# Third block's merge in a three-block kernel on one Trainium2 core: the second branch and the output projection in halves of four tiles, the first tiles in a buffer of their own, the residual totalled on VectorE

## The reference, cut to what matters

```
mixed = (jax.nn.sigmoid(ga) * (h_a @ w_proj_a[layer])
         + jax.nn.sigmoid(gb) * (h_b @ w_proj_b[layer]))
x = _layernorm(ALPHA * x + mixed @ w_out[layer], ln1_g[layer], ln1_b[layer])

ffn = (jax.nn.silu(x @ w_ffn_gate[layer]) * (x @ w_ffn_up[layer])) @ w_ffn_down[layer]
x = _layernorm(ALPHA * x + ffn, ln2_g[layer], ln2_b[layer])
```

## Time and profile before

| | us |
|---|---|
| median of 3 runs | 4739.69 |
| lowest, highest | 4737.83, 4743.4 |
| the profiled execution's own time | 4738.33 |
| its span, first to last instruction | 4736.5 |
| TensorE busy, share of the span | 4343.9, 92% |
| VectorE busy | 2453.9, 52% |
| GpSimd busy | 1295.0, 27% |
| ScalarE busy | 1322.5, 28% |
| mean granted TensorE clock | 0.951 of full |

### The profile page before, as it was taken

How to read it: one execution, slowest core, us unless ns; L and a number is a source line. 1 busy time by engine, 2 the same in 40 slices (tenths; PEclk the granted TensorE clock), 3 DMA queues, 4 the chain that set the end, 5 groups by cost and what they waited for, 6 DMA issues and landing times. The chain is left out here.

```text
span 4736.5 us, 55353 instructions
## 1 busy us (share of the span) xinstructions
PE 4343.9 (92%) x22174; PEld 3377.4 (71%) x22174; DVE 2453.9 (52%) x3774; ACT 1322.5 (28%) x2079; POOL 1295.0 (27%) x502
## 2 busy tenths in 40 slices
PE   8999999978989998989999999989998887988998
PEld 6766787635658784678888678757776775766876
DVE  5544576336647736467777567554552436122023
ACT  3344233213213324223333333222222111102222
POOL 1001443202114330000000144334553331654432
PEclk9999999979999999889999999989998998989999
DMA  5210222212112222510000212211112111211221
GB/s 168 107 36 19 92 103 89 76 71 89 53 71 90 105 96 90 184 56 35 22 35 21 73 71 106 76 72 72 71 71 75 54 54 36 89 71 71 106 89 54
DMA packets 41294, 357.92 MB, mean 76 GB/s; under 512 B 4275, under 2 KB 4659, under 8 KB 21500
## 3 DMA queue, kind: packets, MB, share of 16 engines
q1 hardware_dynamic: 41084, 354.97, 20.6%
HBM read 333.46 MB, written 21.50 MB: 75 GB/s over the span
## 5 line engine op out<-in xcount | busy, mean ns | idle before, releaser
L192 PE MATMUL banks<-ffn_in_high,ffn_weights_low 128*128 128x512 f32 x2112 | 833.0, 394 | 65.3 <-issue 31.7
L193 PE MATMUL banks<-ffn_in_low,ffn_weights_high 128*128 128x512 f32 x2112 | 828.8, 392 | 0.0
L194 PE MATMUL banks<-ffn_in_high,ffn_weights_high 128*128 128x512 f32 x2112 | 828.2, 392 | 0.0
L260 POOL TENSOR_TENSOR ffn_weights_low<-weight_ring,ffn_weights_high 128x2048 fp32r<-128x2048 f32 x128 | 601.2, 4697 | 824.5 <-ACT ffn_weights_high L337 823.8
L192 PEld LDWEIGHTS banks<-ffn_in_high,ffn_weights_low 128*128 128x128 f32 x2112 | 401.4, 190 | 156.1 <-issue 34.4
L193 PEld LDWEIGHTS banks<-ffn_in_low,ffn_weights_high 128*128 128x128 f32 x2112 | 401.1, 190 | 84.8 <-issue 1.5
L194 PEld LDWEIGHTS banks<-ffn_in_high,ffn_weights_high 128*128 128x128 f32 x2112 | 400.7, 190 | 84.2
L337 ACT ACTIVATE ffn_weights_high<-weight_ring 128x2048 fp32r<-128x2048 f32 x128 | 245.1, 1915 | 582.5 <-PE banks L194 582.4
L192 PE MATMUL banks<-third_x_high,third_weights_low 128*128 128x512 f32 x832 | 332.6, 400 | 61.7 <-POOL third_weights_low L3063 24.5
L438 DVE SCALAR_TENSOR_TENSOR ffn_gate<-ffn_up,columns_sb,ffn_gate 128x511 f32<-128x511 f32 (+1 forms) x132 | 287.2, 2176 | 167.6 <-ACT ffn_value L368 167.6
L3063 POOL TENSOR_TENSOR third_weights_low<-weight_ring,third_weights_high 128x1024 fp32r<-128x1024 f32 x144 | 363.2, 2522 | 11.5
(11 more groups left out here) (543 smaller groups left out, 7943.1 us busy)
## 6 DMA issues: line engine op xcount, KB each, us to landing
weight_ring<-weights SPq DMA_DIRECT2D x144, 2048.0 KB, 7.7
scan_in<-rwkv_operands SPq DMA_DIRECT2D x8, 1280.0 KB, 6.8
rwkv_operands<-rwin_staged SPq DMA_DIRECT2D x24, 256.0 KB, 2.1
scan_in<-rwkv_operands SPq DMA_DIRECT2D x8, 512.0 KB, 3.9
bias_tiles<-bias_rows SPq DMA_DIRECT2D x8, 448.0 KB, 8.8
residual<-x SPq DMA_DIRECT2D x4, 512.0 KB, 7.0
filt_decay<-decay SPq DMA_DIRECT2D x1, 2048.0 KB, 8.1
rwkv_residual<-residual SPq DMA_DIRECT2D x1, 2048.0 KB, 7.4
```

The costliest lines, as they stand in the source:

```text
L192: pe.matmul(out, w[1], x[0], start=start, stop=False, skip_group_check=True)
L193: pe.matmul(out, w[0], x[1], start=False, stop=False, skip_group_check=True)
L194: return pe.matmul(out, w[0], x[0], start=False, stop=stop, skip_group_check=True)
L260: pool.tensor_tensor(parts[1], landed, parts[0].bitcast(F32), ALU.subtract).then_inc(S["split"], 1)
```

## The change

Host side: the second branch's weights are laid out by halves of the output columns, four units of 256 rows by 512 columns for each half, and the output projection's by halves of the input rows, four units of 512 rows by 256 columns for each. Number and size of chunks stay.

In `gated_merge`:

- A buffer `merge_early` (high and low part, four tiles each) takes tiles 0 to 3 of branch a and tiles 0 to 3 of the output projection's input. ScalarE and VectorE fill it for branch a at the start of the block, ahead of the gates. Everything else stays in `x_parts`.
- TensorE waits bank by bank, not for all: at the start of branch a for the sigmoid of bank m, at the start of branch b for the multiply of bank m.
- Branch b is two halves of four units. The first half computes output tiles 0 to 3 over all eight input tiles, the second 4 to 7. VectorE takes up the first half's banks as soon as that half is done.
- The output projection is two halves of four units as well. The first takes input tiles 0 to 3 for all eight output tiles, the second input tiles 4 to 7. Its output banks 2j and 2j+1 are finished at the end of unit 4+j.
- VectorE adds the residual tiles up as they are done (seven adds, into the first tile of `merge_gate`), and TensorE sums that one tile with the matrix of ones still inside the merge's block. VectorE waits for this before the block ends.

In `layer_norm` the sum over eight tiles is left out for `ln1`. `ln2` is as before.

```
-            pe.wait_ge(S["gate_done"], 2 * KT)
-            for t in range(tiles):
-                if t == tiles_a:
-                    pe.wait_ge(S["branch_done"], KT)
+            for t in range(tiles_a):
                 pe.wait_ge(S["split"], gate_units + t + 1)
                 pe.wait_ge(S["tile_split"], t + 1)
                 w = w_parts(gate_units + t)
                 for m in range(KT):
-                    mm = exact_product(pe, G.banks[:, m, :], [x[:, m * P:(m + 1) * P] for x in w], [x[:, t % KT, :] for x in x_parts],
-                                       start=t in (0, tiles_a), stop=t in (tiles_a - 1, tiles - 1))
+                    if t == 0:
+                        pe.wait_ge(S["gate_done"], KT + m + 1)
+                    mm = exact_product(pe, G.banks[:, m, :], [x[:, m * P:(m + 1) * P] for x in w], parts(t),
+                                       start=(t == 0), stop=(t == tiles_a - 1))
                 mm.then_inc(S["used"], 1)
-            pe.wait_ge(S["tile_split"], tiles + KT)
-            for m in range(KT):
-                output(gate_units + tiles + m, m)
+            for u in range(KT):
+                half = u // HALF
+                w = [x.rearrange("p (k n) -> p k n", k=2) for x in w_parts(unit_b + u)]
+                pe.wait_ge(S["split"], unit_b + u + 1)
+                for s in range(2):
+                    k = u % HALF * 2 + s
+                    pe.wait_ge(S["tile_split"], tiles_a + k + 1)
+                    for m in range(half * HALF, (half + 1) * HALF):
+                        if k == 0:
+                            pe.wait_ge(S["branch_done"], m + 1)
+                        mm = exact_product(pe, G.banks[:, m, :], [x[:, s, m % HALF * P:(m % HALF + 1) * P] for x in w], parts(tiles_a + k),
+                                           start=(k == 0), stop=(k == KT - 1))
+                mm.then_inc(S["used"], 1)
+            for u in range(KT):
+                w = [x.rearrange("p (k n) -> p k n", k=HALF) for x in w_parts(unit_out + u)]
+                pe.wait_ge(S["split"], unit_out + u + 1)
+                for s in range(HALF):
+                    k = u // HALF * HALF + s
+                    pe.wait_ge(S["tile_split"], tiles + k + 1)
+                    for side in range(2):
+                        m = u % HALF * 2 + side
+                        if k == 0:
+                            pe.wait_ge(S["branch_done"], KT + m + 1)
+                        mm = exact_product(pe, G.banks[:, m, :], [x[:, s, side * P:(side + 1) * P] for x in w], parts(tiles + k),
+                                           start=(k == 0), stop=(k == KT - 1))
+                mm.then_inc(S["used"], 1)
+            pe.wait_ge(S["totalled"], KT - 1)
+            pe.matmul(G.banks[:, 0, :], G.con("ones"), total, start=True, stop=True).then_inc(S["total_summed"], 1)
...
             for m in range(KT):
-                dve.wait_ge(S["used"], gate_units + tiles)
+                dve.wait_ge(S["used"], unit_b + (HALF if m < HALF else KT))
                 dve.tensor_tensor(G.hT[:, m, :], G.banks[:, m, :], G.hT[:, m, :], ALU.mult).then_inc(S["branch_done"], 1)
                 dve.wait_ge(S["branch_done"], KT + m + 1)
                 dve.tensor_tensor(G.hT[:, m, :], G.hT[:, m, :], gates[0][:, m, :], ALU.add).then_inc(S["mixed"], 1)
-            for k in range(KT):
-                tile_low(tiles + k)
+                if m % HALF:
+                    tile_low(tiles + m - 1)
+                if m % HALF == HALF - 1:
+                    tile_low(tiles + m)
             for m in range(KT):
-                dve.wait_ge(S["used"], gate_units + tiles + m + 1)
+                dve.wait_ge(S["used"], unit_out + HALF + m // 2 + 1)
                 dve.scalar_tensor_tensor(out=G.x[:, m, :], in0=G.x[:, m, :], scalar=ALPHA, in1=G.banks[:, m, :],
                                          op0=ALU.mult, op1=ALU.add).then_inc(S["added"], 1)
+                if m:
+                    dve.wait_ge(S["added"], m + 1)
+                    if m > 1:
+                        dve.wait_ge(S["totalled"], m - 1)
+                    dve.tensor_tensor(total, G.x[:, 0, :] if m == 1 else total, G.x[:, m, :], ALU.add).then_inc(S["totalled"], 1)
+            dve.wait_ge(S["total_summed"], 1)
...
-    layer_norm(G, "ln1", "ln1_g", "ln1_b")
+    layer_norm(G, "ln1", "ln1_g", "ln1_b", total_summed=True)
```

More of the change, by code:

```diff
@@ L3631, in gated_merge @@
     nc = G.nc
+    HALF = KT // 2
     tiles_a, tiles_b = M_HEADS * MT_, H_HEADS
@@ L3634, in gated_merge @@
     gate_units = 2 * KT
-    units = gate_units + tiles + KT
+    unit_b = gate_units + tiles_a
+    unit_out = unit_b + KT
+    units = unit_out + KT
     with ExitStack() as ctx:
-        S = stage(G, "merge", ctx, "restored", "rounded", "split", "used", "tile_high", "tile_split", "gate_done", "branch_done", "mixed", "added")
+        S = stage(G, "merge", ctx, "restored", "rounded", "split", "used", "tile_high", "tile_split", "gate_done", "branch_done", "mixed", "added",
+                  "totalled", "total_summed")
         gates = [G.sb("merge_gate", [P, KT, SEQ], ctx=ctx), G.hT]
+        early = [G.sb("merge_early_" + part, [P, HALF, SEQ], F32R, ctx=ctx) for part in ("high", "low")]
+        total = gates[0][:, 0, :]
         x_parts = [T.x_high, T.x_low]
@@ L3646, in source, with parts @@
             return T.haT[:, t, :] if t < tiles_a else T.hbT[:, t - tiles_a, :] if t < tiles else G.hT[:, t - tiles, :]
+        def parts(t):
+            return [x[:, t % KT, :] for x in (early if t < HALF or tiles <= t < tiles + HALF else x_parts)]
         @block.sync
@@ L3659, in _ @@
                     pool.wait_ge(S["used"], n - 1)
[L3660 to L3664 removed]
+                if n >= gate_units:
+                    split_unit(pool, S, G.ring[:, G.slot(c), n % 4 * UNIT:(n % 4 + 1) * UNIT], w_parts(n), n)
+                else:
+                    split_unit(pool, S, column_unit(G, c, n % 4), [w.rearrange("p (k n) -> p k n", k=KT) for w in w_parts(n)], n)
         @block.tensor
         def _(pe):
[L3668 to L3675 removed]
             for t in range(gate_units):
@@ L3679, in _ @@
                     pe.wait_ge(S["gate_done"], t - 7)
[L3680 to L3684 removed]
+                pe.wait_ge(S["split"], t + 1)
+                w = [x.rearrange("p (k n) -> p k n", k=KT) for x in w_parts(t)]
+                for k in range(KT):
+                    mm = exact_product(pe, G.banks[:, t % 8, :], [x[:, k, :] for x in w], [x[:, k, :] for x in x_parts],
+                                       start=(k == 0), stop=(k == KT - 1))
+                mm.then_inc(S["used"], 1)
+            for t in range(tiles_a):
                 pe.wait_ge(S["split"], gate_units + t + 1)
@@ L3698, in tile_high @@
             def tile_high(t):
-                act.activation(x_parts[0][:, t % KT, :], source(t), ACT.Copy).then_inc(S["tile_high"], 1)
+                act.activation(parts(t)[0], source(t), ACT.Copy).then_inc(S["tile_high"], 1)
+            for t in range(HALF):
+                tile_high(t)
             for t in range(2 * KT):
@@ L3706, in _ @@
             act.wait_ge(S["restored"], KT)
-            for t in range(tiles):
+            for t in range(HALF, tiles):
                 if t >= KT:
@@ L3761, in _ @@
         def _(pe):
-            for k in range(KT):
-                mm = pe.matmul(G.banks[:, 0, :], G.con("ones"), G.x[:, k, :], start=(k == 0), stop=(k == KT - 1))
-            mm.then_inc(S["summed"], 1)
+            if not total_summed:
+                for k in range(KT):
+                    mm = pe.matmul(G.banks[:, 0, :], G.con("ones"), G.x[:, k, :], start=(k == 0), stop=(k == KT - 1))
+                mm.then_inc(S["summed"], 1)
             for k in range(KT):
```

22 lines of the change are left out of this document (13 added, 9 removed).

## The result

| us | before | changed |
|---|---|---|
| median, 20 runs each | 4742.09 | 4710.9 |
| lowest, highest | 4731.99, 4748.25 | 4696.99, 4775.71 |
| profiled execution, own time | 4738.33 | 4708.93 |
| span | 4736.5 | 4707.0 |
| ratio, 95% interval | | 0.9949 [0.9928, 0.9969] |

What follows compares the result with a forecast made beforehand. TensorE, busy 92% of the span, was taken as the bound, losing time at stops and slow clock; 5.9 + 6.6 + 18.9 + 2.2 = 33.6 us off 4738.33 gave 4704.7, median 4706, stated 4705; range 4699 to 4711, stretched to 4712.

Steps and rivals of the forecast that it cites:

- Gates to branch a: Joint from gates to branch a: first tiles split early, sigmoid awaited bank by bank, TensorE runs through; minus 5.9 us.
- Branch a to b: Joint from branch a to b: TensorE waits for one multiply, not eight, 0.9 us rest left, no slow start; minus 6.6 us.
- Branch b to output: Joint from branch b to output projection: VectorE and ScalarE finish tiles while the halves run, nothing waits; minus 18.9 us.
- The end: Layer norm's start: one product with ones for eight, earlier mean, part given back in slower squares; minus 2.2 us.
- the least of my three values for the end: At the layer norm, single product and squares both slow: 1.1 us won; the others were 3.9 and 2.2.
- the dear restart: At branch b's start, TensorE restarting slowly after its rest would make the forecast 2.6 us worse.
- GpSimd becoming the bound: Rival: behind the halves, GpSimd's weight splits, slowed beside VectorE, hold TensorE up, up to 5 us; 4710 us, chance 0.10.
- come back at half size: Rival: a tile or bank of the output's first half is late, costing about half of 17.3 us; about 4714 us, chance 0.05.
- fall from lack of rest: Rival: in branch b and output, TensorE without rest drops to clock 0.50; about 4790 us, chance 0.02.

Runs made afterwards that it cites:

- no_early_a: The changed kernel with the early buffer used for the output projection alone, branch a's first four tiles split after the gates; median 4713.56 us.
- b_waits_all: The changed kernel, but TensorE begins branch b only when all eight multiplies are done; 4713.49 us (one run).
- b_whole: The changed kernel with branch b as before (one input tile for all eight outputs) and only the output projection in halves; median 4716.46 us.
- out_waits_all: The changed kernel, but TensorE begins the output projection only when all eight input tiles are split; median 4719.09 us.
- joints_only: The changed kernel with the old layer-norm sum: no adds into a total, eight products with ones inside the layer norm; median 4706.92 us.
- tail_only: The kernel before with only the new end: total on VectorE, one product with ones, none in the layer norm; median 4737.29 us.
- three_products: The changed kernel, but TensorE sums the total of residual tiles 0 to 5, then tiles 6 and 7, with the ones matrix; median 4708.91 us.

## Why the prediction was right and where it was wrong

Three of the four terms were right, mechanism and size; the fourth, the end, was not.

*Gates to branch a* (minus 5.9): 11.38 - 5.44 = 5.94 measured, and its cause by no_early_a.

*Branch a to b* (minus 6.6): 13.00 - 6.57 = 6.43. The rest of 0.9 us is 0.88 in the trace. The products ran at the full clock behind it (1.00 from 4180 to 4184 us), as taken from the rests of 1.04 and 2.17 us. By b_waits_all and the kernel before, the clock is a quarter to a third of what the full wait costs (1.6 of 5.7, 2.6 of 7.6 us).

*Branch b to output* (minus 18.9): 24.38 - 5.44 = 18.94. VectorE's long operations came out longer than the longest I had seen (2.91 us for 2.14) and all of them stayed hidden, four tiles in 15.5 us.

*The end* (minus 2.2) is **the step that failed**: 17.88 us before against 17.97, so nothing won, 0.1 us lost. The wait for VectorE was right (2.83 us for 2.8). The single product ran at the low clock (2.08 us; I had taken 1.0 and kept 2.07 as a bound), the way from its end to the mean took 0.95 us where I had 0.44 from another block's barrier, and the squares took 9.56 us where I had 8.83. These are 1.1, 0.5 and 0.7 us, the 2.3 us between forecast and result. Even the least of my three values for the end, 1.1 us won, was too good by 1.2. With the same end, three profiles (the changed kernel twice, b_whole) have the product at 2.08 us and the end at 17.8 to 18.0; three others (no_early_a, out_waits_all, b_waits_all) have 1.32 to 1.45 us and 16.4. The rest ahead of it was 2.83 us each time, so how much of the product is slow is a matter of when the clock falls, and in the changed kernel the end is worth 0 to 1.5 us. Why it falls earlier in some is open.

Sum: 5.94 + 6.43 + 18.94 - 0.1 = 31.2 us, the measured stretch, where the prediction said 33.6. Its time of 4705 is 5.9 us below the median measured: 2.4 us lie in the stretch, nearly all of it the end, another 2.4 in the kernel before, whose median is 4742.09 over 20 runs and was 4739.69 over the three that I started from, and the last 1.1 in rounding and parts outside the change.

*The range* was made badly too. Its own terms add up to 4700.9 to 4710.3, or 4712.4 with the dear restart, and not to 4699 to 4711. For the runs it allowed 3.7 us above the median, from three runs; the 20 of the changed kernel lie from 14 us below theirs to 65 above. That the median of 4710.9 is inside and the time by the ratio, 4718, outside is decided by these runs and not by the mechanism.

*The rivals.* GpSimd becoming the bound did not happen: after the start of the merge TensorE never waited for a unit. GpSimd's subtract takes 2.75 us beside such operations of VectorE and 2.43 otherwise, VectorE's operation up to 2.91 for 0.68; VectorE pays. The Trainium skill (SBUF — State Buffer, "SBUF: two separate sides") has an exclusive lock on the port pair that the two share, which whoever starts first holds for its whole instruction. The rows agree, with GpSimd as the holder: VectorE's low part that began at 4231.24, 0.39 us after GpSimd's subtract, ended 0.54 us after it, and VectorE's operations are short in out_waits_all where GpSimd has nothing to do. The joint did not come back at half size. The clock did not fall from lack of rest: 83 us at 1.00. The Trainium skill (TensorE: Matmul & The Clock Gate, "A second HAM failure mode: psum-queue depth-cycling") has the clock go down and up again and again where TensorE idles shortly between groups of products. Nothing of that is seen in the merge. At the end the clock fell once, at about 4270.4 us, and was back at 1.00 by 4281, so the place was right but not the pattern, and the least value that I took from that rule was still 1.2 us too good.

## What to carry to other kernels

Where an all-or-nothing wait stands between two stages, cost it as the distance between two of its neighbours' starts less a calm unit; that takes in the slow restart, and with what rest stays taken off it was right to 0.2 us three times here. What a wait put back would cost can't be read off the rows of the kernel that lacks it (12.7 us measured in out_waits_all for the 17 to 18 expected), since the other engines' operations change their durations when TensorE stands still. Halves of the last stage hide work at its joint, but here they finish outputs in pairs and so put one more operation behind the last product. Taking work from an engine that clocks down when it rests can be worth nothing: count what its next work costs at the lower clock, and if a spare product or two fill the rest, try them.

## What was not expected of the hardware

The squares ran slowly in every profile where at most three products with ones stood between the projection and a rest of 2.67 or 3.08 us (8.6 to 9.6 us for sixteen instructions), and not behind eight and a rest of 2.17 us (7.13 us, in the kernel before and in joints_only). Whether the shorter rest or the more work ahead of it keeps the clock up was not tried. The leaving of the block took 0.95 us from the end of the single product to the mean in the changed kernel (and in tail_only and out_waits_all) and 0.53 in three_products; why it differs was not tried. VectorE's operations with two inputs in SBUF took up to 2.91 us for 0.68 beside GpSimd's subtract; one that reads a bank and a tile kept its 0.68 us there (4225.79 us, inside a subtract that began at 4225.40).
